# Reordering the preparation of the first stage: the memory's key and value products, the chunk turns, the scale matrices and the row turns

## The reference, cut to what matters

```python
h = rmsnorm(x, norm_mix[0])                      # S5 mixer, 64 groups of 16 channels, 64 complex states
a_bar = jnp.exp(lam * dt)
b_bar = ((a_bar - 1.0) / lam)[..., None] * lax.complex(b_re, b_im)
bu = jnp.einsum('blgh,gph->blgp', ug, b_bar)
_, states = lax.associative_scan(_ssm_combine, (a_seq, bu), axis=1)
y = jnp.einsum('blgp,ghp->blgh', states, c).real + d_skip * u
...
kv = rmsnorm_2(mem, g_mem) @ w_kv                # memory: 256 rows, 256 key and 256 value columns
```

## Time and profile before

| | us |
|---|---|
| time, median of 3 runs | 1849.71 (1849.65 to 1849.82) |
| the profiled execution, its own time | 1851.44 |
| its span, first to last instruction | 1849.6 |
| TensorE busy | 1811.3 |
| VectorE busy | 1139.9 |
| ScalarE busy | 832.7 |
| GpSimd busy | 732.6 |

### The profile page before, as it was taken

How to read it: one execution, slowest core, us unless ns; L and a number is a source line. 1 busy time by engine, 2 the same in 40 slices (tenths; PEclk the granted TensorE clock), 3 DMA queues, 4 the chain that set the end, 5 groups by cost and what they waited for, 6 DMA issues and landing times.

```text
span 1849.6 us, 24587 instructions
## 1 busy us (share of the span) xinstructions
PE 1811.3 (98%) x9676; PEld 1457.9 (79%) x9676; DVE 1139.9 (62%) x1671; ACT 832.7 (45%) x1351; POOL 732.6 (40%) x430
## 2 busy tenths in 40 slices
PE   7999999999999999999999999999999999999998
PEld 5778888888887688668888888887776768888886
DVE  8953336547475698853355474732636558787878
ACT  6762533323245435765333333353467464343434
POOL 1224343443424378543433434243245443324222
PEclk9999999999999999999999999999999999999999
DMA  4464442341412222004423314125210223415041
GB/s 188 86 155 92 137 137 69 114 125 35 145 38 75 69 92 92 24 24 120 154 69 114 114 46 137 46 83 156 59 66 24 80 93 112 132 52 170 12 137 46
DMA packets 195534, 171.82 MB, mean 93 GB/s; under 512 B 15914, under 2 KB 169002, under 8 KB 195034
## 3 DMA queue, kind: packets, MB, share of 16 engines
q1 hardware_dynamic: 193122, 166.45, 30.0%
q10 hardware_dynamic: 2296, 3.78, 0.6%
HBM read 163.10 MB, written 2.65 MB: 90 GB/s over the span
## 4 chain that ended last, share of the span: by engine, by line
PE 91%; ACT 3%; DVE 3%; issue 1%; POOL 1%; DMA 0%; POOLq 0%; DVEq 0%; ACTq 0%
PE PS L2657 79%; PE PS L3019 2%; PE PS L3010 2%; PE PS L3029 2%; PE PS L2528 1%; PE PS L2571 1%; DVE taken L2364 1%; PE PS L2969 1%; PE PS L2936 0%; ACT probs_t L1461 0%; ACT u L1001 0%; PE PS L2520 0%; PE PS L2586 0%; PE PS L2580 0%; ACT sq_junk L1118 0%
## 5 line engine op out<-in xcount | busy, mean ns | idle before, releaser
L786 POOL TENSOR_TENSOR w_lo<-raw,w_hi 128x2048 fp32r<-128x2048 f32 x92 | 430.2, 4676 | 604.1 <-ACT w_hi L1064 582.5
L2657 PE MATMUL PS<-xT_hi,w_hi 128*128 128x512 f32 (+1 forms) x1160 | 444.7, 383 | 3.1 <-DVE xT_lo L1893 2.0
L2657 PE MATMUL PS<-xT_lo,w_hi 128*128 128x512 f32 (+1 forms) x1160 | 441.9, 381 | 0.0
L2657 PE MATMUL PS<-xT_hi,w_lo 128*128 128x512 f32 (+1 forms) x1160 | 441.7, 381 | 0.0
L1064 ACT ACTIVATE w_hi<-raw 128x2048 fp32r<-128x2048 f32 x105 | 201.2, 1917 | 332.3 <-PE PS L2657 325.0
L2657 PEld LDWEIGHTS PS<-xT_hi,w_hi 128*128 128x128 f32 x1160 | 217.9, 188 | 49.8 <-issue 8.6
L2657 PEld LDWEIGHTS PS<-xT_lo,w_hi 128*128 128x128 f32 x1160 | 217.8, 188 | 42.1
L2657 PEld LDWEIGHTS PS<-xT_hi,w_lo 128*128 128x128 f32 x1160 | 217.9, 188 | 41.3
L793 POOL TENSOR_TENSOR w_lo<-dn_raw,w_hi 128x1024 fp32r<-128x1024 f32 (+1 forms) x46 | 123.5, 2706 | 262.6 <-ACT w_hi L1229 262.6
L2657 PE MATMUL PS<-w_hi,xT_hi 128*128 128x512 f32 (+1 forms) x560 | 220.2, 393 | 1.5 <-issue 1.5
L2657 PE MATMUL PS<-w_hi,xT_lo 128*128 128x512 f32 (+1 forms) x560 | 216.8, 387 | 0.0
(11 more groups left out here) (411 smaller groups left out, 2766.1 us busy)
## 6 DMA issues: line engine op xcount, KB each, us to landing
raw<-in_ffn_w_gate_up SPq DMA_DIRECT2D x88, 512.0 KB, 5.0
dn_raw<-in_ffn_w_down SPq DMA_DIRECT2D x22, 1024.0 KB, 7.9
raw<-in_w_up SPq DMA_DIRECT2D x32, 512.0 KB, 5.4
dn_raw<-in_w_down SPq DMA_DIRECT2D x16, 1024.0 KB, 7.6
raw<-in_dsa_w_in SPq DMA_DIRECT2D x28, 512.0 KB, 4.3
raw<-in_w_in SPq DMA_DIRECT2D x21, 512.0 KB, 5.1
raw<-in_s_w_glu SPq DMA_DIRECT2D x32, 256.0 KB, 4.9
raw<-in_dsa_w_o SPq DMA_DIRECT2D x8, 512.0 KB, 4.0
```

The lines of the kernel that those rows point to most:

```text
L786: pool.tensor_tensor(w_lo[:, g % 2, :], raw[:, r % 2, :], f32(w_hi[:, g % 2, :]), ALU.subtract).then_inc(w_split, 1)
L2657: ins = mm(o, a if weights_stay else c, c if weights_stay else a, start=first and n == 0, stop=last and n == 2, skip_group_check=onto)
```

## The change

On TensorE `kv_keys(1)` goes ahead of the swap, and `kv_values(1)` behind `kv_values(0)`; both values wait, as before, for `s5_bs`. Then come `u_turn` of batches 0 to 3, a wait for both copies of `kv`, `u_turn` of batch 4, `s5_in_turn(0)`, a wait for its copy, `u_turn` of batches 5 and 6, `s5_in(0)`, `s5_lags(0)`, `u_turn` of batch 7 and `s5_in_turn(1)`. On ScalarE `mem_diag` stands ahead of the two sines, rows 0 to 4 ahead of the `b_s` copies, and rows 5 to 7 behind `pw_is`; then both `kv` copies, `table(0)`, the copy of turn 0, `in_map_out(0)`, the copies of turns 1 to 7, and `lag_out(0)`. On VectorE `chunk_turns` stands ahead of `input_map(0)`. The banks of the turns are dealt out anew.

```diff
--- before.py
+++ after.py
@@ -39,7 +39,7 @@
 TABS = 4
 SEEDED = [0 < b < NB - 1 for b in range(NB)]
 CQ = CH // 2
-TURN_BANKS, U_EARLY = [5, 1, 6, 2, 3, 0, 7, 6], 5
+TURN_BANKS, U_EARLY = [5, 1, 6, 0, 7, 2, 3, 6], 5
 
 
 HD = 64
@@ -973,13 +973,14 @@
                 if m:
                     act.wait_ge(mem_sq, 1)
                 act.activation(mem_junk[:, :], mem[:, m, :], ACT.Square, accum_out=ssq[:, 32 + m:33 + m]).then_inc(mem_sq, 1)
+            act.wait_ge(mem_rstd, 1)
+            for m in range(2):
+                act.activation(mem_diag[:, m, :], ident[:, :], ACT.Copy, scale=rstd[:, 32 + m:33 + m]).then_inc(mem_scale, 1)
+
             act.wait_ge(s5_ang, 1)
             act.activation(small[:, 12, :], small[:, 11, :], ACT.Sin).then_inc(s5_sin, 1)
             act.activation(small[:, 13, :], small[:, 11, :], ACT.Sin, scale=0.5).then_inc(s5_sin, 1)
             act.wait_ge(ld_late, 16)
-            act.wait_ge(mem_rstd, 1)
-            for m in range(2):
-                act.activation(mem_diag[:, m, :], ident[:, :], ACT.Copy, scale=rstd[:, 32 + m:33 + m]).then_inc(mem_scale, 1)
 
             def mem_turned(i):
 
@@ -1000,11 +1001,10 @@
                     of, at = slice(NC * (s // CQ), NC * (s // CQ) + NC), s % CQ
                     act.activation(u[:, :, s, :], xp[of, at, :].rearrange("p (g h) -> p g h", h=GH), ACT.Copy, scale=rstd[of, at:at + 1]).then_inc(s5_u, 1)
 
-            rows_scaled(0, 2)
+            rows_scaled(0, 5)
             act.wait_ge(s5_swap, 1)
             act.activation(b_s[:, 0:G // 2, :].rearrange("p g h -> p (g h)"), PS[:, 0, :], ACT.Copy)
             act.activation(b_s[:, G // 2:G, :].rearrange("p g h -> p (g h)"), PS[:, 7, :], ACT.Copy).then_inc(s5_bs, 1)
-            rows_scaled(2, 3)
             act.wait_ge(s5_pw, 1)
             act.activation(pw_is[:, :, :], pw_i[:, :, :], ACT.Copy, scale=sign[:, 1:2]).then_inc(s5_pw_is, 1)
 
@@ -1023,7 +1023,7 @@
                 act.wait_ge(s5_cos, 2 * n + 1)
                 act.activation(tab_c[rows, gs, :], turns[rows, of, :], ACT.Sin, bias=quarter[rows, :], scale=-6.283185).then_inc(s5_cos, 1)
 
-            rows_scaled(3, CH)
+            rows_scaled(5, CH)
 
             def gelu(b):
                 act.wait_ge(s5_y, b + 1)
@@ -1071,20 +1071,19 @@
                     act.activation(uT[:, GB * q:GB * q + GB, :].rearrange("p g c -> p (g c)"), PS[:, TURN_BANKS[q], :], ACT.Copy).then_inc(s5_ut_sb, 1)
 
             kv_copy(0)
-            in_map_out(0)
-            turned_rows(0, U_EARLY)
+            kv_copy(1)
             act.wait_ge(s5_u, CH)
             table(0)
+            turned_rows(0, 1)
+            in_map_out(0)
+            turned_rows(1, NB)
             lag_out(0)
             decay_out(0)
             in_map_out(1)
-            kv_copy(1)
             for b in range(NB - 1):
                 if b == 0:
                     table(1)
                 lag_out(b + 1)
-                if b == 0:
-                    turned_rows(U_EARLY, NB)
                 if b == NB - 2:
                     act.wait_ge(s5_v, NB)
                     round_slot(0)
@@ -1835,8 +1834,8 @@
 
 
             dve.wait_ge(s5_pw, 1)
+            chunk_turns()
             input_map(0)
-            chunk_turns()
             dve.wait_ge(ld_c, 16 * 2)
             output_map(0)
             input_map(1)
@@ -2488,12 +2487,12 @@
 
             pe.wait_ge(ld_kvw, 16)
             kv_keys(0)
+            kv_keys(1).then_inc(kv_done, 1)
             pe.wait_ge(s5_bn, 1)
             pe.wait_ge(ld_rot, 16)
             for b in range(2):
                 ins = mm(PS[:, 7 * b, :], rot[:, 2 * P:3 * P], b_n[:, 32 * b:32 * b + 32, :].rearrange("p g h -> p (g h)"), start=True, stop=True)
             ins.then_inc(s5_swap, 1)
-            kv_keys(1).then_inc(kv_done, 1)
 
             def kv_values(m):
 
@@ -2504,6 +2503,7 @@
             pe.wait_ge(ld_kvv, 16)
             pe.wait_ge(s5_bs, 1)
             kv_values(0)
+            kv_values(1).then_inc(kv_done, 1)
 
             def s5_out_at(b, side, g):
 
@@ -2586,8 +2586,6 @@
                 mm(PS[:, 5, :], rot[:, P:2 * P], sz[:, :, :].rearrange("p g c -> p (g c)"), start=False, stop=True,
                    skip_group_check=True).then_inc(s5_x, 1)
 
-            s5_in_turn(0)
-
             def u_turn(first, last):
 
                 for q in range(first, last):
@@ -2596,16 +2594,19 @@
                     ins.then_inc(s5_ut, 1)
 
             pe.wait_ge(s5_u, CH)
-            u_turn(0, 3)
+            u_turn(0, U_EARLY - 1)
+            pe.wait_ge(kv_sb, 2)
+            u_turn(U_EARLY - 1, U_EARLY)
+            s5_in_turn(0)
             pe.wait_ge(s5_int_sb, 1)
-            u_turn(3, U_EARLY)
-            pe.wait_ge(kv_sb, 1)
-            kv_values(1).then_inc(kv_done, 1)
-            pe.wait_ge(ld_c, 16 * 2)
-            s5_lags(0)
+            u_turn(U_EARLY, NB - 1)
             pe.wait_ge(s5_ut_sb, 1)
             s5_in(0)
-            pe.wait_ge(s5_ut_sb, U_EARLY)
+            pe.wait_ge(ld_c, 16 * 2)
+            pe.wait_ge(s5_ut_sb, 4)
+            s5_lags(0)
+            u_turn(NB - 1, NB)
+            pe.wait_ge(s5_ut_sb, NB - 1)
             s5_in_turn(1)
             def s5_turn(i):
 
@@ -2623,10 +2624,6 @@
                 s5_in(b + 1)
                 if b + 2 < NB:
                     s5_lags(b + 1)
-                if b == 0:
-                    pe.wait_ge(s5_lag_sb, 1)
-                    pe.wait_ge(kv_sb, 2)
-                    u_turn(U_EARLY, NB)
                 if b + 2 < NB:
                     s5_in_turn(b + 2)
                 else:
```

## The result

| | before | changed |
|---|---|---|
| median of 20 runs, us | 1850.98 (1849.65 to 1852.48) | 1856.41 (1850.43 to 1859.46) |
| profiled execution, its own time | 1851.44 | 1857.36 |
| span | 1849.6 | 1855.6 |
| mean granted clock of the profiled execution | 0.998 | 0.994 |

The ratio is 1.0028, interval 1.0022 to 1.0034: the changed kernel is slower by 0.3%, 5.4 us between the medians. With twenty runs the kernel before has its median at 1851.0, 1.3 us above the three runs shown first. The single times of the changed kernel go with the mean granted clock: 1850.43 at 0.999, 1852.03 and 1852.47 at 0.998, between 1856.67 and 1859.46 for the five executions at 0.994.

The account below looks back on a forecast made before the run. TensorE's unbroken work was taken to bound the kernel, its start following the first rotation at 49.11 us. Rotation 0.9 us sooner, 0.2 given back: 0.7 us faster, median 1849.71 to 1849.0; range 1847.0 to 1852.8.

Parts of the forecast that it names:

- The scale matrices: mem_diag ahead of the sines: ScalarE's work from first square to row scale 1.8 us sooner, first row at 24.4; held safe.
- The new idle before the values: TensorE stands 2.9 us for the b_s copies; the clock was expected to fall within the values, costing 1.5 us.
- ScalarE up to the tables: ScalarE stands 4.4 us for the values; table(0) starts at 40.25 as before, so moving chunk turns first gains nothing.
- rival A: The clock doesn't fall in the new idle before the values; gain 2.4 - 0.6 to 2.4 us, 1847.7; chance 0.15.
- The weak stretch behind the values: TensorE from 39.65 to 46.1: turns of 64 rows, transposes, a 1.4 us stand, turns again; feared only as rival B.
- rival B: A second clock fall, behind the values, low clock granted by 46 us: costs 3.0 us, 1852.0; chance 0.22.
- 9.5 us pass that VectorE and GpSimd set and that the change leaves alone: The stretch from the first rotation at 49.11 to TensorE's unbroken work at 58.6, taken as unchanged.
- I count both as even up to the chain's entry ... VectorE may wait a few tenths. I take 0.2: Behind the first rotation: later lags against fewer TensorE turns in batch 0 are even; the late second table costs 0.2 us.
- The last sentence of the prediction: Wrong if the first rotation comes sooner but batches 1 to 3 give it back waiting for taps or tables.
- The range: 8 in 10 for 1847.0 to 1852.8, covering A, C, the forecast and B up to a second low stretch about the first's size.

Follow-up runs that it names:

- the run with the idle filled: Changed kernel with table copies ahead of the taps transfers, three added matmuls before turns 5 and 6, six before the values: 1849.17 us.
- the lags ahead of the copy of turn 7: Changed kernel with lag_out(0) and decay_out(0) ahead of the copy of turn 7 on ScalarE, nothing else: 1854.12 us, ratio 1.0019.
- the tables ahead: Changed kernel with the table copies ahead of the wait for the lags and the taps transfers in SyncE's queue: 1852.72 us, ratio 1.0011.
- the filler alone: Changed kernel with three never-read matmuls of 256 columns where TensorE stands 1.6 us for in_t: 1851.84 us, ratio 1.0009.
- the order drawn anew: Changed kernel with keys 1 cut around the swap, s5_in(0) before turns 5 and 6, ScalarE reordered, tables first in SyncE's queue, five fillers: 1847.52 us.
- the filler in the kernel before: Kernel before with three never-read matmuls of 256 columns where TensorE stood 1.57 us before the turns: 1851.8 us, ratio 1.0005.
- filler and tables: Changed kernel with both the three added matmuls before turns 5 and 6 and the table copies ahead of the taps transfers: 1849.96 us, ratio 0.9996.
- the new order without fillers: The version at 1847.52 us without its five added matmuls, the order alone: 1850.43 us, ratio 0.9996 to the kernel before.

## Why the prediction was wrong

**The scale matrices: right.** First square at 16.12 (16.1 forecast), released by the rows' transfer. First row scaled at 24.05 instead of 24.4, since GpSimd's two instructions for the scale took 0.3 us less. Alone the part has a median 0.7 us better and a ratio of 1.0006, which is no change clear of noise.

**The new idle before the values: right in place and size, its price open in both directions.** It was 2.72 us (2.9), released by the `b_s` copy. In the profiled execution the clock did not fall there, and the values took 7.14 us; in the profiles of three of the experiments, with the same code up to there, it did, and they took 8.83. The 1.5 us of the forecast lie close to that 1.7. The price in the median is 0.8 us by the run with the idle filled.

**ScalarE up to the tables: right.** It stood for the values, which held the table and not the chunk turns, 2.80 us instead of 4.4. Without the fall `table(0)` began at 38.40, 1.85 us before the 40.25 forecast: the 1.5 us of rival A and the 0.35 us of the first row.

**The weak stretch behind the values: the first step that failed.** The prediction had the pattern as rival B with a chance of 0.22 and a price of 3.0 us for a low stretch of 6.8 us. It came in two of the three profiles of kernels that keep this idle of 1.60 us (the changed kernel and the lags ahead of the copy of turn 7, not the tables ahead), and the stretch was 10.2 us. Turns 5 and 6 took 1.93 us, `s5_in(0)` 3.67 us (1.6 us more, as priced). That the first rotation came at 48.66, near the 48.2 forecast, is luck: `in_t` was ready 2.0 us sooner than worked out, since the clock had not fallen in the values, and the turns and `s5_in(0)` took 2.5 us longer, since it fell behind them.

**"9.5 us pass that VectorE and GpSimd set and that the change leaves alone".** This failed with the fall. From the first rotation to the rotation out of batch 0 it took 10.4 us, with TensorE busy to the end: 0.45 us ahead of the kernel before became 0.4 us behind. In the profiles without a low clock in this stretch it took 9.5 us (the tables ahead, the filler alone, the order drawn anew); with one, 10.1 (the lags ahead of the copy of turn 7), 10.3 (the filler in the kernel before), 10.8 (filler and tables) and 12.0 (the new order without fillers). Still, the changed kernel was only 0.4 us late by then. Without what followed, the profiled execution would have been within measurement of the kernel before.

**"I count both as even up to the chain's entry ... VectorE may wait a few tenths. I take 0.2": the second step that failed, and the large one.** The late `lag_out(1)` was seen, and its way through SyncE's queue to the second table too. It was forecast at 58.1 and ended at 59.8 with the low clock; the copy took 5.2 us, not 3.6 to 4.2; VectorE waited 2.9 us and TensorE 2.1. And the wait was priced as a wait. Behind it came a low stretch of 6.8 us, in a stage that had run at full clock: from L2580 to the rotation out of batch 2 TensorE took 7.9 us where it had taken 4.8. So 2.1 + 3.1 = 5.2 of the 6.0 us are made here, where the sum had 0.2. The last sentence of the prediction named this as what would make it wrong, but gave it no chance of its own.

**The range.** It was drawn as if the clock fell in the same place each time; three runs of before agreed to 0.2 us and gave no hint that it does not. Twenty runs of it spread over 2.8 us and twenty of the changed kernel over 9.0, and the 1849.0 forecast lies below the fastest of either. Of that, 1.3 us are the base, whose median is 1851.0 and not 1849.71; the forecast gain of 0.7 us against the measured loss of 5.4 is the same miss on either base.

**Why slower, in one line:** both regroupings make TensorE stand, the clock can come down behind each idle, and the second table, whose place in the queue stayed behind the lags of batch 1, comes after the moment it is wanted, which makes one more idle and often one more low stretch. The queue and the second idle are shown by their repairs, 3.7 and 4.6 us alone and 6.5 together. Not shown are the price of each regrouping alone on the kernel before, since no run has it, and that it matters that the turns have 64 rows, since no run changes them. The version at 1847.52 shows that an order of this kind can win; it changes several things at once, and apart from the fillers, without which 2.9 of its 3.5 us are gone, they aren't separated.

## What to carry to other kernels

In this kernel an idle of TensorE of 1 to 3 us had two prices, the idle and what the low clock took behind it; the second could be the larger (2.1 and 3.1 us in batch 2), it differed between executions, and a few matmuls of no use in the idle were cheaper than it where TensorE itself held the stage. Take the price from the stage's end and not from the low time, of which much can be hidden. Follow every moved copy to the transfers it releases, and through the order of their queue to the next thing that somebody waits for; issue a transfer when its data is ready, not where its loop stands; a stage that moves forward needs its transfers to move with it. And fill an idle only if what follows isn't held by something else, or it opens again at the next wait.

## What the runs showed of the hardware that was not expected

- The low clock's place isn't a property of the kernel. The same code up to the values, with the same idle of 2.7 us, kept 2.4 GHz in the profiles of the changed kernel and of the one with filler and tables (1.0 up to 53 us), and went to 1.2 GHz at about 31 us in three others.
- The length of the idle didn't decide it. The last idle ahead of a fall was 0.93 us (filler and tables), 0.94 (the scale matrices alone), 1.57, 1.60 and 2.09 (changed), 1.79 (the new order without fillers) and 2.64 (the filler in the kernel before); the same two idles of 0.94 and 1.60 us, and others of 1.67, 2.39 and 2.43 us, passed without one in other profiles.
- A low stretch can hold long under unbroken work: in the changed kernel TensorE was busy for all of 44 to 53 us at 0.5, with turns, matmuls with 64 columns and lags with 16 columns. Low stretches lasted between 3.4 and 13.7 us.
- Nine added matmuls and an edit of the queue brought the changed kernel from 1856.41 to 1849.17 and its spread from 9.0 to 1.2 us.
- A copy of 256 KB between the partition halves landed 3.6 us after its issue for the first table. For the second table, with a store of 512 KB just ahead of it in the same queue, it took 4.2 us in the kernel before and with the scale matrices alone, where the next `taps` transfers are issued 3.8 to 4.1 us behind it, and 5.0 to 5.4 us in the changed kernel and four others, where they are issued 1.5 to 3.2 us behind it. No run varies this alone, so that these transfers slow the copy isn't shown.
